# A decoder trunk's prologue on one core: high halves of the first units ahead of the modulated tiles, and conditioning tiles moved between the steps of layer 0

## The chip, the cores and the metric

The kernel runs on one core of one Trainium2 chip. The metric is the device time of one execution in microseconds (us). Times here come from repeated runs of the kernel and from one profiled execution. A core has TensorE (PE in the profile, its weight loads PEld), VectorE (DVE), ScalarE (ACT), GpSimd (POOL) and SyncE (SP), which here issues most transfers.

## The reference, cut to what matters

Two layers over 256 rows of width 2048, batch one. The conditioning vector c gives shift, scale and gate of both sub-layers through w_ada (2 x 2048 x 12288):

```
cond = silu(c)
for l in range(2):
    ada = cond @ w_ada[l] + b_ada[l]
    sh_m, sc_m, g_m, sh_f, sc_f, g_f = split(ada, 6)
    h = x * (1 + sc_m) + sh_m
    y = hybrid_mixer(h, ...)      # h @ w_in (6672 columns), three head groups, @ w_out
    x = layer_norm(alpha * x + (1 + g_m) * y)
    h = x * (1 + sc_f) + sh_f
    y = square(relu(h @ w1[l])) @ w2[l]
    x = layer_norm(alpha * x + (1 + g_f) * y)
```

The mixer's three groups are a retention, a gated linear recurrence (HGRN2, with masks at several levels) and a state space layer (Mamba-2) whose input goes through a causal convolution of four taps.

## The kernel before

**Units and passes.** Every weight matrix is read in units of 128 x 1024 f32 (0.5 MB). A layer has 25 passes of 16 units, 400 units; unit n belongs to pass n // 16. Passes 0 to 6 are the input projection (pass 3 has 528 columns only), 7 and 8 the output projection, the rest the MLP. A matmul in full precision is made of three: each weight W is split into a high half WH (ScalarE rounds it to fp32r, `hi_split`, line 735) and a low half WL = W - WH (VectorE subtracts, `lo_split`, line 1116), and each left operand likewise. Both splits run four units (`AHEAD`) in front of the matmuls. RAW and WL share nine slots, WH has six; SyncE loads unit n when unit n - 9 has been multiplied, and ScalarE's high half of unit n needs unit n - 6 multiplied.

**Conditioning tiles.** A tile is 128 of the columns of w_ada, turned, 128 x 2048 f32 (1 MB). VectorE makes its 128 values with one multiply-and-accumulate over 2048 elements, a dot. 32 tiles (shift and scale of the first sub-layer) are needed before the first matmul; they are the prologue. The other 160 are spread over the steps of VectorE's program: `tile_plan()` lists at which unit each dot stands, gives the tile one of seven slots (ONE, XA, XB, HA, HB, HC, KM) and the unit behind whose weights SyncE issues the tile's load, at least three units later in the order of the queue and at least eight behind the dot that last used the slot. HA to HC are free only when passes 0 to 6 are done, and x itself is loaded (by GpSimd, at unit 114) over the slots XA and XB when their last dot, at unit 112, is done.

**The prologue.** Eight batches b. In each, VectorE does four dots (`first_dot`, line 1347), makes the scale and shift columns of two tiles of h (`first_cols`, lines 1354 and 1355), then subtracts the low halves of the batch's first units (`FIRST_UNITS[b]`: two in batches 0 to 4, four in 5 to 7) and the low parts of the two tiles (`h_lo`, line 1122). Batches 1 and 2 hold small tables too. ScalarE does `first_tiles(b)`: two tiles of h, each written twice (lines 772 and 775), which wait for the columns; then the high halves of the batch's units. The matrix engine multiplies the batch's units (line 1643 for those of pass 0, 1675 for those of pass 1). SyncE issues the four tiles of a batch into four slots, each when the dot four before it is done, a 0.5 MB piece of the turned x in every second batch, and then the batch's units.

**The steps around the tiles.** Each engine's program goes through the units in order with the other work written in at fixed places. On VectorE a step does: a mask of the recurrence (`hg_mask`, lines 1333 to 1341; passes 2 and 3, units 7, 10, 13 and 15 of each), the low half of the unit four ahead, then the dots of that step (`dot`, line 1057), then the convolutions (pass 3, units 52, 53, 55, 56, 58, 59, 61, 62, and pass 4, units 67 to 70), and the rest of the head groups (line 1504: eight products of pass 5; lines 1536 and 1544: norm of the third group, pass 7). ScalarE and the matrix engine have their own lists, with semaphores between them. `GATE_DUE` says at which unit the matrix engine turns eight tiles' values into half a gate (`gate_sums`, line 1605); VectorE reads the sums two steps later (`gate_out`, line 1066), and the matrix engine waits for that three steps later. In layer 0 the second gate half of the mixer is due at unit 140, so the wait stands at 143, ahead of the last four units of pass 8, which are multiplied together by row and column quarter (`last_units`, line 1657).

Of the kernel before, what the change touches and what calls it, by code (L numbers as in the profile page):

```python
# [17 lines left out]
P = 128  # L18
# [6 lines left out]
UW = 1024  # L25
# [3 lines left out]
FIRST_UNITS = [[(0, 2 * b), (0, 2 * b + 1)] + ([(1, 2 * (b - EARLY_FROM)), (1, 2 * (b - EARLY_FROM) + 1)] if b >= EARLY_FROM else []) for b in range(8)]  # L29
# [15 lines left out]
LN_EPS, RMS_EPS = 1e-5, 1e-6  # L45


GATE_DUE = [{125: 4, 140: 5, 172: 10, 195: 11}, {106: 16, 134: 17, 172: 22, 195: 23}]
GATE_SEQ = [4, 5, 10, 11, 16, 17, 22, 23]
LATE = 14  # L50
ONE, XA, XB, HA, HB, HC, KM = range(7)
# [2 lines left out]
def tile_plan():  # L54

    both = [t for kt in range(KT) for t in (48 + kt, 64 + kt)]
    plan = [(0, [23, 25, 27, 29, 31, 33, 35, 37, 40, 42, 44, 46, 50, 55, 60, 66, 71, 76, 80, 83, 85, 88, 91, 94,
                 96, 98, 101, 103], both[:2 * LATE]),
            (0, [105, 107, 109, 112, 114, 117, 119, 121], range(32, 40)),
            (0, [124, 126, 128, 130, 132, 134, 136, 138], range(40, 48)),  # L60
            (0, [145, 148, 151, 154], both[2 * LATE:]),
            (0, [156 + 2 * k for k in range(8)], range(80, 88)),
            (0, [174 + 5 * k // 2 for k in range(8)], range(88, 96)),
            (0, [196 + 49 * k // 16 for k in range(64)],
             [96 + t for kt in range(KT) for t in (kt, 16 + kt)] + [96 + t for t in both]),
            (1, [80 + 3 * k for k in range(8)], [96 + t for t in range(32, 40)]),
            (1, [107 + 3 * k for k in range(8)], [96 + t for t in range(40, 48)]),
            (1, [145 + 3 * k for k in range(8)], [96 + t for t in range(80, 88)]),
            (1, [174 + 5 * k // 2 for k in range(8)], [96 + t for t in range(88, 96)])]
    tiles, last, uses = [], {}, {}  # L70
    for layer, steps, cols in plan:
        for n, t in zip(steps, cols):
            step, i = layer * NUNIT + n, 32 + len(tiles)
            if n >= FF0 * KT:
                slots = (ONE, KM)
            elif n >= 117:
                slots = (ONE, HA, HB, HC)
            else:
                slots = (ONE, XA, XB) if layer == 0 and n <= 112 else (ONE,)
            slot = min(slots, key=lambda k: last.get(k, (-1, 0))[0] if k in last else -1)  # L80
            prev = last.get(slot)
            load = max(step + 3, prev[0] + 8 if prev else 0, layer * NUNIT + 121 if HA <= slot <= HC else 0,
                       tiles[-1][4] if tiles else 0)
            assert load <= step + 11, (step, load)
            fresh = slot >= HA and (prev is None or prev[0] < layer * NUNIT + 112)
            uses[slot] = uses.get(slot, 0) + 1
            tiles.append((step, t, slot, uses[slot], load, prev[1] if prev else None, fresh))
            last[slot] = (step, i)
    return tiles
# [15 lines left out]
COL0 = [2048, 3072, 5120, 6144, 0, 1024, 4096]  # L105
# [43 lines left out]
def hybrid_trunk(nc, x, c, positions, lb_logits, w_in, w_out, w_ada, b_ada, ln_g, ln_b, hg_norm_w,  # L149
                 m_conv_w, m_conv_b, m_dt_bias, m_a_log, m_d, m_norm_w, w1, w2, consts, x_turned, out):  # L150
    with ExitStack() as ctx:
# [280 lines left out]
        w_in_r = w_in.rearrange("l k n -> (l k) n")  # L432
# [101 lines left out]
        @block.sync  # L534
        def _(sp):
            def tile_load(layer, i):
                _, t, slot, _, _, prev, fresh = TILES[i - 32]
                if prev is not None:
                    sp.wait_ge(dots.sem, prev + 1)
                if fresh:  # L540
                    sp.wait_ge(unit_done.sem, unit_done.at(layer, 7 * KT))
                sp.dma_start(tile_slot(i), w_ada_r[t]).then_inc(tile_in[slot].sem, 16)

            def raw_load(layer, n, src):
                slot = raw_slot(layer, n)
                if layer or n >= RAW_SLOTS:
                    sp.wait_ge(unit_done.sem, unit_done.at(layer, n + 1) - RAW_SLOTS)
                if len(src.shape) == 3:
                    dst = RAW[:, slot, :].rearrange("p (t n) -> p t n", t=2)
                else:  # L550
                    dst = RAW[:, slot, 0:src.shape[1]]
                sp.dma_start(dst, src).then_inc(raw_in[slot].sem, 16)

            sp.dma_start(CROW[:, :], c.squeeze(0).partition_broadcast(P)).then_inc(pro_crow.sem, 16)
            n = 0
            for b in range(8):
                for i in range(4 * b, 4 * b + 4):
                    if i >= PRO_SLOTS:
                        sp.wait_ge(dots.sem, i - PRO_SLOTS + 1)
                    sp.dma_start(FT[:, i % PRO_SLOTS, :], w_ada_r[i % 2 * 16 + i // 2]  # L560
                                 ).then_inc(pro_tile[i % PRO_SLOTS].sem, 16)
                    if i % 8 == 0:
                        t0 = i // 2
                        sp.dma_start(XT[:, t0:t0 + 4, 1, :], x_turned[t0 * P:(t0 + 4) * P, :].rearrange(
                            "(t p) n -> p t n", p=P)).then_inc(pro_xt.sem, 16)
                for p, kt in FIRST_UNITS[b]:
                    raw_load(0, n, w_in_r[kt * P:(kt + 1) * P, COL0[p]:COL0[p] + UW])
                    n += 1
            for layer in range(DEPTH):
                for p in range(FF0):  # L570
                    for kt in range(KT):
                        n = p * KT + kt
                        if layer == 0 and n < EARLY:
                            continue
                        if p < 7:
                            src = w_in_r[ds(layer * D + kt * P, P), COL0[p]:COL0[p] + width(p)]
                        else:
                            src = w_out_r[ds(layer * D + OUT_ORDER[kt] * P, P), (p - 7) * UW:(p - 6) * UW]
                        raw_load(layer, n, src)
                        for i in LOAD_AT.get(layer * NUNIT + n, ()):  # L580
                            tile_load(layer, i)
                for g in range(GROUPS):
                    for m in range(4 * KT):
                        s, kt = divmod(m, KT)
                        n = FF0 * KT + g * 64 + m
                        if split_unit(g, m):
                            src = w1_r[ds(layer * D + m % 8 * 2 * P, 2 * P), ds(g * D + m // 8 * 512, 512)
                                       ].rearrange("(t p) n -> p t n", p=P)
                        elif s < 2:
                            src = w1_r[ds(layer * D + kt * P, P), ds(g * D + s * UW, UW)]  # L590
                        else:
                            src = w2_r[ds(layer * DFF + g * D + kt * P, P), (s - 2) * UW:(s - 1) * UW]
                        raw_load(layer, n, src)
                        for i in LOAD_AT.get(layer * NUNIT + n, ()):
                            tile_load(layer, i)
            for i in range(8):
                r, ch = divmod(i, 4)
                sp.wait_ge(x_out.sem, i + 1)
                cols = slice(ch * 512, (ch + 1) * 512)
                sp.dma_start(out_r[:, r, cols], X[:, r, cols]).then_inc(out_done.sem, 16)  # L600
            sp.wait_ge(out_done.sem, 16 * 8)
# [97 lines left out]
        def _(act):  # L699
# [173 lines left out]
            act.activation(ACT_IDLE[:, :], PT[:, 0:1], ACT.Identity)  # L873
            n = 0
            for b in range(8):
                first_tiles(b)
                for _ in FIRST_UNITS[b]:
                    hi_split(0, n)
                    n += 1
                if b == 1:  # L880
                    act.wait_ge(pro_dve.sem, 1)
                    act.activation(LX[:, :], LX[:, :], ACT.Exp).then_inc(pro_act.sem, 1)
                    act.wait_ge(pro_dve.sem, 2)
                    act.activation(SIN[:, :, :], ANG[:, :, :], ACT.Sin).then_inc(pro_act.sem, 1)
                    act.activation(S2[:, :, :], ANG[:, :, :], ACT.Sin, scale=0.5).then_inc(pro_act.sem, 1)
            for n in range(EARLY, EARLY + AHEAD):
                hi_split(0, n)
            for layer in range(DEPTH):
                for p in range(FF0):
                    for kt in range(KT):  # L890
                        n = p * KT + kt
# [25 lines left out]
                        if p in (2, 3) and kt in HG_X1:  # L917
                            i = (p - 2) * 4 + HG_X1.index(kt)
# [9 lines left out]
                        if p in (2, 3) and kt in HG_M and HG_M.index(kt) % 2:  # L928
                            i = (p - 2) * 4 + HG_M.index(kt)
# [35 lines left out]
                        if p == 5 and kt in M_ARG:  # L965
                            i = M_ARG.index(kt)
# [42 lines left out]
                for g in range(GROUPS):  # L1009
# [15 lines left out]
                    for m in range(4 * KT):  # L1025
                        s, kt = divmod(m, KT)
                        n = FF0 * KT + g * 64 + m
# [989 lines left out]
```

## Time and profile before

| | us |
|---|---|
| median of 3 runs (lowest, highest) | 2494.16 (2489.54, 2495.68) |
| the profiled execution | 2494.9 |
| its span, first to last instruction | 2493.1 |
| PE busy | 2374.6 (95%) |
| DVE busy | 1898.1 (76%) |
| ACT busy | 1158.9 (46%) |
| POOL busy | 173.2 (7%) |

The span is what the trace covers; the time of the execution is 1.8 us more. A busy share is an average: the matrix engine is busy through nearly all stages and stands still in a few places, which the rows below show. Transfers moved 637.97 MB, 256 GB/s on average.

### The profile page before, as it was taken

The page shows a single profiled execution, that of the slowest core. Times are in us where ns is not written, and L with a number is a line of the kernel's source. Part 1 is how long each engine was busy: PE and PEld are TensorE (multiplying, and loading weights), DVE is VectorE, ACT ScalarE, POOL GpSimd, SP SyncE. Part 2 cuts the span into 40 slices and gives each one's busy share as a digit, 9 for nine tenths or more (in the row PEclk, how much of TensorE's full clock was granted, in tenths as well). Part 3 has the DMA queues.
Part 4 walks back from the last instruction along what each step waited for, and adds up shares of the span by engine and source line. Part 5 has one row for each costly group of instructions (what it writes and reads, how often), then busy time and mean ns, then how long its engine had stood idle before and what let it go on. Part 6 is the DMA issues. An engine that isn't in the chain of part 4 may idle for free.

```text
span 2493.1 us, 31995 instructions
## 1 busy us (share of the span) xinstructions
PE 2374.6 (95%) x12916; PEld 2055.3 (82%) x12916; DVE 1898.1 (76%) x2128; ACT 1158.9 (46%) x1505; POOL 173.2 (7%) x122
## 2 busy tenths in 40 slices
PE   2589999999999999999999999999999999999998
PEld 2579888778888888888879998888888888888886
DVE  5878987888998878888886578777888565655657
ACT  2254565635434434434446447554553443443442
POOL 0002100010011011020010110001001101101001
PEclk9799999999999999999999999999999999999999
DMA  8996677978999888888866446677788656656653
GB/s 343 368 344 232 208 262 265 336 301 283 341 354 319 304 322 310 311 318 312 310 195 184 146 121 210 228 272 258 267 283 288 190 189 194 186 190 192 186 192 118
DMA packets 179912, 637.97 MB, mean 256 GB/s; under 512 B 17260, under 2 KB 20020, under 8 KB 153780
## 3 DMA queue, kind: packets, MB, share of 16 engines
q1 hardware_dynamic: 174928, 617.94, 71.7%
q0 software_dynamic: 3296, 17.43, 1.9%
q8 instruction: 102, 1.67, 0.3%
q10 hardware_dynamic: 1540, 0.55, 0.1%
q14 instruction: 46, 0.38, 0.1%
HBM read 633.75 MB, written 2.10 MB: 255 GB/s over the span
## 4 chain that ended last, share of the span: by engine, by line
PE 86%; DVE 9%; ACT 2%; issue 1%; DMA 1%; ACTq 0%; DVEq 0%
PE PS L1675 44%; PE PS L1701 17%; PE PS L1703 9%; PE PS L1643 6%; PE PS L1684 4%; DVE WL L1116 3%; PE PS L1657 2%; DVE FT L1347 2%; DVE FH L1057 1%; DMA MD<-in_m_d 1%; ACT WH L735 1%; PE PS L1734 1%; DVE CV L1322 1%; PE PS L1626 0%; PE PS L1605 0%
## 5 line engine op out<-in xcount | busy, mean ns | idle before, releaser
L1116 DVE TENSOR_TENSOR WL<-RAW,WH 128x1024 fp32r<-128x1024 f32 (+1 forms) x800 | 995.7, 1256 | 494.3 <-ACT WH L735 492.5
L735 ACT ACTIVATE WH<-RAW 128x1024 fp32r<-128x1024 f32 (+1 forms) x800 | 829.9, 1043 | 1035.8 <-PE PS L1675 533.2
L1701 PE MATMUL PS<-HT,WH 128*128 128x512 f32 x1792 | 633.4, 399 | 0.0
L1703 PE MATMUL PS<-HT,WL 128*128 128x256 f32 x1792 | 503.1, 281 | 0.0
L1701 PEld LDWEIGHTS PS<-HT,WH 128*128 128x128 f32 x1792 | 336.7, 188 | 83.6
L1675 PE MATMUL PS<-WH,T2h 128*128 128x512 f32 x1208 | 373.3, 390 | 3.2 <-DVE T2l L1122 3.2
L1675 PE MATMUL PS<-WH,T2l 128*128 128x512 f32 x1208 | 372.7, 390 | 0.0
L1675 PE MATMUL PS<-WL,T2h 128*128 128x512 f32 x1208 | 372.6, 390 | 0.0
L1703 PEld LDWEIGHTS PS<-HT,WL 128*128 128x128 f32 x1792 | 338.5, 189 | 0.2
L1675 PE MATMUL PS<-WH,HT 128*128 128x512 f32 x1024 | 287.6, 394 | 0.6 <-issue 0.6
L1675 PEld LDWEIGHTS PS<-WH,T2h 128*128 128x128 f32 x1208 | 226.0, 188 | 50.5 <-DVE T2l L1122 4.1
L1675 PEld LDWEIGHTS PS<-WH,T2l 128*128 128x128 f32 x1208 | 227.2, 188 | 47.4
L1675 PEld LDWEIGHTS PS<-WL,T2h 128*128 128x128 f32 x1208 | 227.1, 188 | 47.4
L1675 PEld LDWEIGHTS PS<-WH,HT 128*128 128x128 f32 x1024 | 188.4, 188 | 38.8 <-issue 0.9
L1643 PE MATMUL PS<-HT,WH 128*128 128x256 f32 x1024 | 154.8, 303 | 66.0 <-DVE WL L1116 64.5
L623 POOL TENSOR_TENSOR X<-X,Y 128x512 f32<-128x512 f32 x64 | 113.9, 1811 | 1327.4 <-DVE Y L1280 1327.4
L1643 PEld LDWEIGHTS PS<-HT,WH 128*128 128x128 f32 x1024 | 142.2, 209 | 69.9 <-DVE WL L1116 66.7
L1057 DVE SCALAR_TENSOR_TENSOR FONE<-FONE,CROW 128x2048 f32<-128x2048 f32 x77 | 178.1, 2313 | 0.4 <-DMA FONE<-in_w_ada 0.3
L1675 PE MATMUL PS<-WL,HT 128*128 128x512 f32 x512 | 158.2, 390 | 0.0
L1684 PE MATMUL PS<-HT,WH 128*128 128x256 f32 x768 | 143.7, 287 | 0.0
L1684 PEld LDWEIGHTS PS<-HT,WH 128*128 128x128 f32 x768 | 120.0, 192 | 0.2
L1057 DVE SCALAR_TENSOR_TENSOR FK<-FK,CROW 128x2048 f32<-128x2048 f32 x50 | 115.3, 2306 | 0.1
(293 smaller groups left out, 2125.6 us busy)
## 6 DMA issues: line engine op xcount, KB each, us to landing
RAW<-in_w SPq DMA_DIRECT2D x512, 512.0 KB, 4.5
RAW<-in_w_in SPq DMA_DIRECT2D x192, 512.0 KB, 3.8
FONE<-in_w_ada SPq DMA_DIRECT2D x77, 1024.0 KB, 7.0
FK<-in_w_ada SPq DMA_DIRECT2D x50, 1024.0 KB, 6.9
FT<-in_w_ada SPq DMA_DIRECT2D x32, 1024.0 KB, 7.0
RAW<-in_w_out SPq DMA_DIRECT2D x64, 512.0 KB, 6.7
FX<-in_w_ada SPq DMA_DIRECT2D x21, 1024.0 KB, 6.1
FH<-in_w_ada SPq DMA_DIRECT2D x12, 1024.0 KB, 10.1
```

What stands on the lines that cost most here:

```text
L623: pool.tensor_tensor(xc, xc, Y4[:, b, :], ALU.add).then_inc(x_add.sem, 1)
L735: act.activation(WH[:, wh_slot(layer, n), 0:w], RAW[:, k, 0:w], ACT.Copy).then_inc(hi_done.sem, 1)
L1057: stt(w, w, 1.0, CROW[:, :], ALU.mult, ALU.mult, accum_out=ADA[:, ds(t, 1)]).then_inc(dots.sem, 1)
L1116: tt(WL[:, k, 0:w], RAW[:, k, 0:w], WH[:, wh_slot(layer, n), 0:w].bitcast(F32), ALU.subtract).then_inc(lo_done.sem, 1)
L1322: ins = stt(dst[:, j, sh:SEQ], src[:, j, 0:SEQ - sh], cCW[:, tap, t:t + 1], dst[:, j, sh:SEQ], ALU.mult, ALU.add)
L1347: stt(w, w, 1.0, CROW[:, :], ALU.mult, ALU.mult, accum_out=ADA[:, ds(i % 2 * 16 + i // 2, 1)]).then_inc(dots.sem, 1)
L1643: ins = mm(dst, w[:, slot[w is WL], j * P:(j + 1) * P], a[:, kt, :], start=first and i == 0 and j % 2 == 0, stop=last and i == 2, skip_gro ...
L1657: ins = mm(bank(p, q)[:, :], a[:, kt, rows], w[:, slot[w is WL], h * 512:(h + 1) * 512], start=False, stop=n == units[-1] and i == 2)
L1675: ins = mm(bank(p, 2 * r + h)[:, :], a[:, kt, rows], w[:, slot[w is WL], h * 512:(h + 1) * 512], start=first and i == 0, stop=last and i == 2)
L1684: ins = mm(dst, w[:, slot[w is WL], cols], a[:, kt, :], start=first and i == 0 and j % 2 == 0, stop=last and i == 2, skip_group_check=True)
L1701: mm(bank(p, j)[:, :], WH[:, wh, cols], HT[:, kt, :, :], start=kt == 0, stop=False, skip_group_check=True)
L1703: ins = mm(bank(p, j)[:, SEQ:2 * SEQ], WL[:, wl, cols], HTh[:, kt, :], start=False, stop=kt == KT - 1, skip_group_check=True)
```

## The change

Four edits. ScalarE makes the high halves of a batch's units before the batch's modulated tiles, not after them. SyncE issues a batch's units between its second and third tile (i % 4 == 1) and not behind its fourth. In layer 0, the 44 dots up to unit 138 are spread anew: fifteen stand up to unit 49 where thirteen stood up to 50, none between 50 and 65 (before: 50, 55, 60), and those of 66 to 138 now stand at 66 to 130, closer together, with the loads and slots that the planner derives from them. The second gate half of the mixer in layer 0 is due at unit 134 and not 140. Layer 1 keeps its steps.

```diff
-GATE_DUE = [{125: 4, 140: 5, 172: 10, 195: 11}, {106: 16, 134: 17, 172: 22, 195: 23}]
+GATE_DUE = [{125: 4, 134: 5, 172: 10, 195: 11}, {106: 16, 134: 17, 172: 22, 195: 23}]
...
-    plan = [(0, [23, 25, 27, 29, 31, 33, 35, 37, 40, 42, 44, 46, 50, 55, 60, 66, 71, 76, 80, 83, 85, 88, 91, 94,
-                 96, 98, 101, 103], both[:2 * LATE]),
-            (0, [105, 107, 109, 112, 114, 117, 119, 121], range(32, 40)),
-            (0, [124, 126, 128, 130, 132, 134, 136, 138], range(40, 48)),
+    plan = [(0, [23, 25, 27, 29, 31, 32, 33, 35, 36, 39, 42, 45, 47, 48, 49, 66, 70, 77, 79, 81, 83, 85, 87, 89,
+                 92, 94, 96, 98], both[:2 * LATE]),
+            (0, [100, 101, 103, 106, 107, 109, 111, 112], range(32, 40)),
+            (0, [117, 118, 120, 121, 123, 124, 126, 130], range(40, 48)),
...
-                for p, kt in FIRST_UNITS[b]:
-                    raw_load(0, n, w_in_r[kt * P:(kt + 1) * P, COL0[p]:COL0[p] + UW])
-                    n += 1
+                    if i % 4 == 1:
+                        for p, kt in FIRST_UNITS[b]:
+                            raw_load(0, n, w_in_r[kt * P:(kt + 1) * P, COL0[p]:COL0[p] + UW])
+                            n += 1
...
             for b in range(8):
-                first_tiles(b)
                 for _ in FIRST_UNITS[b]:
                     hi_split(0, n)
                     n += 1
+                first_tiles(b)
```

## Rows read from the trace of the kernel before

**Rows 1.** Waits of PE, whole run: us in total, times, longest us.
```profile
PE PS L1643 <- DVE WL L1116: 64.5, 8, 15.9
...
PE PS L1657 <- issue: 3.4, 1, 3.4
```

**Rows 2.** Timeline of the prologue: start us, us, engine, line, operation, [idle before].
```profile
26.70 0.20 ACT L728 ACTIVATE AL<-AL 16x2 f32<-16x2 f32 x1 [9.48 <-DMA MD<-in_m_d]
...
29.93 2.36 DVE L1116 TENSOR_TENSOR WL<-RAW,WH 128x1024 fp32r<-128x1024 f32 x2 [7.56 <-ACT WH L735]
...
32.88 2.29 DVE L1347 SCALAR_TENSOR_TENSOR FT<-FT,CROW 128x2048 f32<-128x2048 f32 x1
...
41.92 0.15 DVE L1355 SCALAR_TENSOR_TENSOR SC<-ADA,PT 128x2 f32<-128x2 f32 x1
...
44.09 1.99 ACT L735 ACTIVATE WH<-RAW 128x1024 fp32r<-128x1024 f32 x2
45.16 2.36 DVE L1116 TENSOR_TENSOR WL<-RAW,WH 128x1024 fp32r<-128x1024 f32 x2 [3.09 <-ACT WH L735]
...
137.79 2.29 DVE L1347 SCALAR_TENSOR_TENSOR FT<-FT,CROW 128x2048 f32<-128x2048 f32 x1
...
140.00 2.29 DVE L1347 SCALAR_TENSOR_TENSOR FT<-FT,CROW 128x2048 f32<-128x2048 f32 x1
...
145.65 4.63 DVE L1116 TENSOR_TENSOR WL<-RAW,WH 128x1024 fp32r<-128x1024 f32 x4 [3.09 <-ACT WH L735]
```

**Rows 3.** Windows: busy us of PE, PEld, DVE, ACT, POOL, granted clock, DMA share, GB/s.
```profile
12.00:34.00 22.00, 3.78 (x17) 3.50 (x18) 11.42 (x15) 5.98 (x10) 0.00 (x0) 1.00 1.01 405
60.00:125.00 65.00, 36.78 (x216) 34.92 (x216) 52.45 (x75) 17.67 (x26) 0.00 (x0) 0.73 0.95 368
90.00:120.00 30.00, 16.49 (x98) 16.00 (x99) 23.76 (x27) 9.83 (x14) 0.00 (x0) 0.72 1.01 397
343.30:365.70 22.40, 22.40 (x101) 17.47 (x100) 22.40 (x22) 14.49 (x22) 0.00 (x0) 1.00 0.86 318
486.90:491.90 5.00, 4.95 (x15) 3.92 (x16) 3.34 (x9) 4.63 (x10) 0.85 (x2) 0.66 0.93 382
549.00:556.00 7.00, 5.54 (x13) 4.41 (x14) 1.25 (x3) 0.00 (x0) 0.00 (x0) 0.52 0.21 88
```

**Rows 4.** Timeline of pass 3 in layer 0, VectorE and the matrix engine.
```profile
257.22 0.93 DVE L1116 TENSOR_TENSOR WL<-RAW,WH 128x528 fp32r<-128x528 f32 x1 [2.27 <-ACT WH L735]
...
278.71 0.49 PE L1748 MATMUL PS<-V,SM 128*128 128x128 f32 x2 [2.83 <-DVE SM L1341]
...
284.95 2.29 DVE L1057 SCALAR_TENSOR_TENSOR FX<-FX,CROW 128x2048 f32<-128x2048 f32 x1
...
290.60 0.49 PE L1748 MATMUL PS<-V,SM 128*128 128x128 f32 x2 [2.46 <-DVE SM L1341]
```

**Rows 5.** Timeline of pass 5: the first product and the matmul that takes it.
```profile
364.86 0.95 DVE L1504 TENSOR_TENSOR MW<-MW,SB 128x768 f32<-128x768 f32 x1
...
366.07 0.43 PE L1878 MATMUL PS<-XD,MW 128*128 128x64 f32 x2
```

**Rows 6.** Timeline of pass 7: the dot of unit 114 and the waits behind it.
```profile
466.39 2.28 DVE L1057 SCALAR_TENSOR_TENSOR FONE<-FONE,CROW 128x2048 f32<-128x2048 f32 x1
...
477.75 1.94 PE L1758 MATMUL PS<-K,XS 128*128 128x128 f32 x16 [1.69 <-DVE XS L1544]
...
480.82 1.06 ACT L735 ACTIVATE WH<-RAW 128x1024 fp32r<-128x1024 f32 x1 [2.71 <-DMA RAW<-in_w_out]
...
486.95 0.73 PE L1675 MATMUL PS<-WH,T2h 128*128 128x512 f32 x2 [1.79 <-DVE T2l L1122]
```

**Rows 7.** Timeline of pass 8: VectorE reads the gate's sums.
```profile
548.97 1.28 DVE L1066 SCALAR_TENSOR_TENSOR GB<-PS,GB 128x512 f32<-128x512 f32 x2
```

**Rows 8.** The chain that ended last: start us, us, what, at two sub-layers' last four units.
```profile
550.46 13.84 PE PS L1657 x48
...
1278.27 10.89 PE PS L1657 x48
```

## Prediction

> **What bounds the kernel now.** I read the waits of the matrix engine first: where it stands still, and for whom, since it is busy for nearly the whole span. The reader is to see one large sum, 64.5 us in eight waits for the low halves of the first weights, and one wait of 3.4 us that the profile puts to nobody [rows 1]; smaller ones stand in passes 3 and 7 of layer 0 [rows 4, 6]. Everything between the eight batches of the prologue and those places is continuous matmul work, so only what moves these waits moves the end. Then I read the timeline at each. In a prologue batch VectorE does four dots of 2.21 us from start to start, the columns, and then stands 3.09 us until ScalarE has made two modulated tiles twice over and the first high half, and only then subtracts; the engine that sets the pace idles for the helper [rows 2]. The windows say what the transfers have left: 397 to 405 GB/s where they are dense, 368 over the batches from 60 to 125 us [rows 3].
>
> **The prologue, ScalarE's order.** With the high halves first, they are ready long before the columns, except in batch 0. What VectorE then does per batch is four dots 8.85, columns 0.25, two subtractions and two tile differences 3.0 (from 29.93 to the next dot at 32.88): 12.1 us where it now takes 15.2. The 3.09 goes from batches 1 to 7. In batch 0 ScalarE is free only at 26.9 us, after the last small table [rows 2]; two high halves (2.0), then four tile operations (2.0) end at 30.9, so the last difference ends at 31.2 and the dots of batch 1 begin there in place of 32.9: 1.6 us. If VectorE alone set the pace, its last dot would end 1.6 + 6 x 3.09 = 20.1 us earlier, at 122.2 in place of 142.3, and the matrix engine would start batch 7 another 3.09 earlier: 23.2 us.
>
> **The prologue, transfers.** A tile of w_ada is 128x2048 f32, 1.05 MB, a first unit 128x1024, 0.52 MB, a quarter of the turned x 0.52 MB. From the ninth tile on there are 24 x 1.05 + 18 x 0.52 + 3 x 0.52 = 36.2 MB until the last tile lands, since the units of a batch now stand ahead of its third and fourth tile in SyncE's queue. The ninth tile can be asked for when the fifth dot is done, 1.6 us earlier than at 35.1 us, so the stream starts at about 35.2. From then on four tile slots are asked for again as the dots go, and in the 3.3 us that VectorE spends on differences up to 4 MB are outstanding: the stream doesn't stop. At 400 GB/s (between the two dense windows of [rows 3]) it takes 90.5 us, the last tile lands at 125.7, its dot ends at 128.0: 14.3 us earlier than now. That is later than VectorE's 122.2, so from about batch 5, where four units are loaded and not two, the tiles set the pace. With the 3.09 of the last batch the matrix engine is 17.4 us earlier in batch 7 and from there on. Bounds: 23.2 (VectorE's pace) and, at 385 GB/s, 94.0 us of stream, 13.9.
>
> The Trainium skill ("DMA: Bandwidth & Descriptors", Specifications) gives about 358 GB/s as a core's HBM limit, which speaks against this change: by it the stream would take 101 us and the gain be 6.8 us. The trace does not agree: its dense windows are above it by a tenth [rows 3].
>
> ScalarE's new order can block: the high half of a batch's last unit needs the slot of the unit six before. In batch 7 that is a unit of batch 6, whose matmuls start some 15 us before batch 7's columns; costed at nothing, and if that unit is late, batch 7 waits the difference. The moved load issues (22 of 0.4 us) stand where SyncE waits for dots anyway.
>
> **Dots out of the convolutions.** Now dots stand at units 50, 55 and 60; the last two lie right before masks for which the matrix engine then waits 2.83 and 2.46 us [rows 4]. With both gone VectorE's chain is 2 x 2.21 = 4.4 us shorter. Against it, three dots now stand at 47, 48, 49 and none at 46 or 50: VectorE would come to the subtraction at 257.2 with 2.9 us more work behind it, but it stands idle 2.27 there, waiting for ScalarE [rows 4]; so it is 0.6 late. That leaves 3.8; bounds 2.2 (one dot's worth) and 5.3, both waits gone.
>
> **Denser dots after them.** Units 66 to 98 now hold one more dot until unit 85: 66, 70, 77, 79, 81, 83, 85 in place of 66, 71, 76, 80, 83, 85. That extra 2.2 us comes ahead of the first product of pass 5, which now ends 0.3 us before the matrix engine takes it [rows 5], and VectorE is busy through the 22 us before [rows 3]. So the matrix engine will wait 1.9 us where it waits nothing now: a loss of 1.9, up to 3.6 if its clock falls as behind the wait in pass 7 [rows 3]. The later products have a wider margin, or a dot less in front of them.
>
> **Pass 7.** The dot of unit 114 stands right before the product that the norm of the third head group needs [rows 6]; moved to 111, it gives the chain 2.2 us, and the wait of 1.69 for the transposed rows goes. But the next one, for the low tiles, is held by ScalarE too, which stands 2.71 us for weights in a dense stretch of transfers, and now two tiles of w_ada are ahead of one of them. I let the low tiles come 2.1 us earlier in all; bounds 0 and 3.9 (both waits and the slow matmuls after them: 5 us at 0.66 granted behind the second wait, so 1.7 lost [rows 3]).
>
> **Pass 8.** Dots at 128, 132, 134, 136, 138 are gone, 11 us of VectorE's work, and the gate's half is summed at unit 134 and read at 136. Now VectorE comes to it only at 549, after all the subtractions [rows 7], and the matrix engine, which may not start its last four units before, waits 3.44. Its granted clock is 0.52 in the stretch behind, near the lower of its levels, 1.2 GHz [rows 3], and the last 48 matmuls take 13.84 us where the same 48 take 10.89 in the next layer boundary [rows 8]. Both go: 3.4 + 2.95 = 6.4, bounds 3.4 and 6.4. The 16 matmuls of the gate's sum are as many as before.
>
> **Costed at nothing.** Other moved dots and their loads: each tile's load is still at least three units behind its dot's, and the weights behind it in the queue have nine slots, 9 x 2.7 us of matmul work (48 matmuls are four units [rows 8]). Were that cover gone, each tile would cost its 1.05 MB at 400 GB/s, 2.6 us. The three moved into passes 2 and 3 fall into idle time of VectorE. Layer 1 has the same steps.
>
> **Sum.** 17.4 + 3.8 - 1.9 + 2.1 + 6.4 = 27.8 us. The profiled execution took 2494.9 (span 2493.1), so 2467.1; the median of the runs is 0.7 lower, which gives 2466.
>
> **Rivals.** (1) VectorE keeps the pace: transfers do better than 400 GB/s. 5.8 us more, 2460; with waits and clock in passes 5 and 7 at their better bounds 2455. For it: the two limits are only 5.8 us apart. Chance 0.2. (2) The stream is slower, since tiles now queue behind units and each dot waits for its own: at the 368 GB/s of the batches now, 98.4 us of stream, 7.9 more, 2474; with the poorer bounds of passes 3, 5 and 7, 2480. For it: the transfer engines are at 0.95 there already [rows 3]. Chance 0.2. The skill's 358 GB/s of the page above would give 2477 in place of 2474. (3) Slower than before, by handshakes. In passes 2, 3 and 5 the matrix engine takes a VectorE result at each of 16 steps; a dot that falls ahead of one costs 2.2 us, and 1.7 more if the clock falls. I find one such; from eight on the whole gain is gone, and eleven give 2507. Against it: in pass 5 the matrix engine waits for none of them now, and most are well ahead. Chance 0.03. (4) The change doesn't do what it says: ScalarE is held by slots or landed weights, so the 3.09 stays. Then 2494 - 10.4 = 2484; chance 0.05. Forecast, 2461 to 2472: 0.52.
>
> **Numbers.** 0.3% is 7.5 us, what a measurement of this kernel can tell from no change. Faster by more: the forecast, (1), (2) and all but a part of (4), 0.95; same 0.02; slower 0.03, from (3). The range reaches to the bounds of (1) and (2): 2455 to 2479.
>
> **What would show it.** In the profile after: VectorE's subtractions in the prologue with no idle time to ScalarE ahead of them from batch 1 on, and some to the tiles' transfers in batches 5 to 7; the eight waits near 47 in place of 64.5; the last dot of the prologue near 128; the masks' waits in pass 3 under 3 us in sum; a new wait of about 2 us for the first product of pass 5; no wait ahead of the last four units of pass 8, and 48 of them in 10.9 us. If the last dot of the prologue ends after 135, the transfers are the reason I am wrong; if pass 5 shows several waits, the denser dots are.

## The result, and the profile after

The changed kernel takes 2480.3 us (median of 5 runs, 2479.1 to 2481.8), 13.9 us less than before; the ratio to before is 0.9949, 95% interval 0.9933 to 0.9964. The forecast was 28 us, 2466 with a range from 2455 to 2479: the direction was right, half of the gain is missing, and the time lies 1.3 us outside the range. The profiled execution spans 2480.0 us, 13.1 less than before. Lines of the changed kernel stand one further than before (1643 is 1644, and so on).

I read the waits of the matrix engine first, then the chain of work that ended last, and took from it the time at which the same matmuls start in both kernels. That gives the gain by stage.

The waits of PE over the whole run (engine, line, what it waited for: us in total, times, longest):

```profile
PE PS L1644 <- DVE WL L1117: 35.5, 7, 7.5
PE PS L1644 <- ACT HT L773: 14.6, 1, 14.6
...
PE PS L1676 <- issue: 7.5, 2, 7.2
PE PS L1749 <- DVE SM L1342: 6.3, 4, 2.1
PE PS L1879 <- DVE MW L1505: 3.5, 3, 1.9
PE PS L1676 <- DVE T2l L1123: 2.9, 2, 1.5
PE PS L1644 <- DVE HT L1123: 2.4, 2, 1.6
```

Against [rows 1]: the waits of the prologue, ten now, are 35.5 + 14.6 + 2.4 = 52.5 us in place of 64.5, and the wait of line 1657 is gone. In its place stands a new one of 7.2 us at line 1676 that the profile puts to nobody ("issue"), and a wait for products of pass 5.

The prologue in the chain of the changed kernel (start us, us, what):

```profile
69.18 11.47 DMA FT<-in_w_ada
...
114.61 12.76 DMA FT<-in_w_ada
...
127.38 2.31 DVE FT L1348 x2
...
129.95 4.54 DVE WL L1117 x4
...
134.88 5.90 PE PS L1644 x32
140.78 19.07 PE PS L1676 x84
```

The chain goes through the tiles' transfers, four times; the last dot ends at 129.7 (before 142.3, [rows 2]). The long run of pass 1 begins at 140.78; in the kernel before it began at 154.78, so 14.0 us are gained here. The same prologue began pass 1 between 138.6 and 140.8 in the traces of runs 1, 5, 6, 7 and 9, so this figure is good to about 2 us.

The timeline of PE at five places, in the order of time, shows where gain goes and comes:

```profile
255.25 0.79 PE L1749 MATMUL PS<-V,SM 128*128 128x128 f32 x2 [2.10 <-DVE SM L1342]
...
352.19 0.43 PE L1879 MATMUL PS<-XD,MW 128*128 128x64 f32 x2 [1.94 <-DVE MW L1505]
...
385.55 0.43 PE L1879 MATMUL PS<-XD,MW 128*128 128x64 f32 x2 [0.76 <-DVE MW L1505]
...
473.27 0.73 PE L1676 MATMUL PS<-WH,T2h 128*128 128x512 f32 x2 [1.47 <-DVE T2l L1123]
...
504.32 1.19 PE L1676 MATMUL PS<-WH,T2h 128*128 128x512 f32 x2 [7.17 <-issue]
```

In pass 3 the wait for a mask stands at 255 and no longer at 279 and 291 [rows 4]; the last mask is taken at 274.71, 15.9 us earlier than in [rows 4]. At the first product of pass 5 (352.19 for 366.07, [rows 5]) 13.9 are left, at line 1898 in pass 6 11.5 (412.11 for 423.58), at the low tiles of pass 7 13.7 (473.27 for 486.95, [rows 6]), and at the gate's sums behind unit 125, where the slow matmuls of [rows 3] lie behind the kernel before, 15.3 (489.73 for 505.01). Then comes the wait of 7.2 us, and the four rows behind it, at 0.50 of the clock, take 1.5 us more than at full clock. Pass 8 ends without a wait, in the chain:

```profile
540.63 10.89 PE PS L1658 x48
```

It ends 12.8 us earlier than in [rows 8], which is what is left of the gain.

What the matrix engine waits for at 504 is read in the same chain, upstream of it:

```profile
476.32 16.34 DMA RAW<-in_w_out
...
493.65 2.85 ACT X L903 x2
...
497.26 1.05 ACT WH L736
...
498.34 0.98 DVE WL L1117
...
499.48 2.29 DVE FH L1058 x2
501.77 1.15 DVE WL L1117
...
504.32 2.04 PE PS L1676 x4
```

The weights of unit 129 take 16.3 us from their issue to landing. Those of unit 128 are late too: ScalarE stands 7.44 us for them, then scales x (3.7 us) ahead of the next high half, and a dot of 2.3 us stands between two subtractions on VectorE. The piece of 1.40 us that the chain calls "issue" has a name in VectorE's timeline (first line ScalarE's, then VectorE's):

```profile
491.48 2.27 ACT L736 ACTIVATE WH<-RAW 128x1024 fp32r<-128x1024 f32 x2 [7.44 <-DMA RAW<-in_w_out]
...
492.57 1.23 DVE L1117 TENSOR_TENSOR WL<-RAW,WH 128x1024 fp32r<-128x1024 f32 x1 [3.71 <-ACT WH L736]
...
502.82 1.28 DVE L1067 SCALAR_TENSOR_TENSOR GB<-PS,GB 128x512 f32<-128x512 f32 x2
```

The last line is VectorE reading the sums of the first gate half, due at unit 125. It does so in step 127, behind the low half of unit 131, and the matrix engine may not start unit 128 before the read is done. The read ends at 504.10, the matmul starts at 504.32. Unit 128's own low half (the line at 492.57) had been there since 493.80, and the matrix engine had come to it at 497.15. So the wait is one for the gate's read, held up by late weights, and not one for the weights of the unit that is multiplied. The other traces bear this out: the read ends and unit 128 starts at 517.58 and 517.82 in run 4, 496.98 and 497.20 in run 5, 497.98 and 498.19 in run 7. In the kernel before the read ended at 511.24 and unit 128 began at 512.27, so there was 1.0 us to spare. The wait ahead of the last four units of pass 8, which the profile also puts to nobody, is of the same kind ([rows 7, 8]: the read ends at 550.25, the matmuls start at 550.46).

The window over this stretch says what the transfers do, 414 GB/s over 50 us at a busy share of 1.01, while the matrix engine works 41 of 50 us (columns as in [rows 3]):

```profile
455.00:505.00 50.00, 41.36 (x197) 34.16 (x196) 40.44 (x50) 27.58 (x42) 1.71 (x4) 0.96 1.01 414
```

### The profile page after: what moved, and what is told of

Same layout as the page of the kernel before. It is cut to its first block, busy times and chain, and to the rows that moved or that the text cites. A ratio compares the mean times of both kernels' runs of the same rounds, so it can differ in the third digit from the quotient of the medians.

```text
span 2480.0 us, 31995 instructions
## 1 busy us (share of the span) xinstructions
PE 2371.3 (96%) x12916; PEld 2052.9 (83%) x12916; DVE 1898.5 (77%) x2128; ACT 1161.7 (47%) x1505; POOL 167.3 (7%) x122
## 4 chain that ended last, share of the span: by engine, by line
PE 84%; DVE 9%; DMA 3%; ACT 1%; issue 1%; ACTq 0%; DVEq 0%
PE PS L1676 42%; PE PS L1702 17%; PE PS L1704 9%; PE PS L1644 6%; PE PS L1685 4%; DVE WL L1117 2%; DMA FT<-in_w_ada 2%; PE PS L1658 2%; DVE FT L1348 1%; DMA MD<-in_m_d 1%; DVE FX L1058 1%; PE PS L1735 1%; DMA RAW<-in_w_out 1%; DVE CV L1323 1%; DVE FONE L1058 1%
## 5 line engine op out<-in xcount | busy, mean ns | idle before, releaser
L1644 PE MATMUL PS<-HT,WH 128*128 128x256 f32 x1024 | 152.6, 300 | 53.9 <-DVE WL L1117 35.5
```

What stands on the lines that cost most here:

```text
L1644: ins = mm(dst, w[:, slot[w is WL], j * P:(j + 1) * P], a[:, kt, :], start=first and i == 0 and j % 2 == 0, stop=last and i == 2, skip_gro ...
```

## The experiments

Each ratio is to the kernel before, measured beside it on the same chip. An interval is about 0.0013 wide to either side, 3 us.

**1 to 4. The prologue alone, its two halves, and the rest alone.** The edits are the hunks of the diff ahead of the prediction:

```diff
e1: kernel before + hunk of SyncE's loads + hunk of ScalarE's order
e2: kernel before + hunk of ScalarE's order
e3: kernel before + hunk of SyncE's loads
e4: changed kernel - these two hunks (GATE_DUE and tile_plan() alone)
```

> The kernel before with both prologue edits (ScalarE's high halves first, SyncE's first units ahead of the third and fourth tile) and nothing else. Theory: the prologue is worth 14.0 us, as the start of the pass behind it shows in the changed kernel (140.78 in place of 154.78), and the rest of the change is worth nothing in sum: 2494.2 - 14.0 = 2480.2, from 2478 to 2482. Rival: the rest of the change is worth several us by itself, since waits moved by the earlier prologue (dots against products) took part of it: then this one is slower than the changed kernel, 2484 or more. Second rival: the rest of the change costs, because the weights of pass 7 come late only with the new list of steps: 2478 or less.

Measured: 2479.6 us, ratio 0.9936 (0.9924 to 0.9949). As the theory said.

> The kernel before with only ScalarE's order changed (high halves ahead of the modulated tiles); the loads stay behind the batch's four tiles. Theory: the units then land some 12 us behind the previous batch's last dot, about when the columns are there, so the high halves start late and hold the tiles back; a part of the gain stays, about 7 us: 2487, 2483 to 2491; the 3.09 us of idle time ahead of VectorE's subtractions shrinks but does not go. Rival: ScalarE's order is all of it, the moved loads are worth nothing: 2480, idle gone.

Measured: 2475.8 us, ratio 0.9923 (0.9909 to 0.9936). Theory and rival were both wrong: ScalarE's order alone gives 19.5 us, more than with the loads moved. In its timeline VectorE, after batch 0, waits for tiles in one batch only, three times, and for ScalarE 0.41 us in each of the last four batches:

```profile
99.79 0.42 DVE L1122 TENSOR_TENSOR HT<-TX,HT 128x256 fp32r<-128x256 f32 x1 [0.41 <-ACT TX L775]
103.22 2.29 DVE L1347 SCALAR_TENSOR_TENSOR FT<-FT,CROW 128x2048 f32<-128x2048 f32 x1 [0.79 <-DMA FT<-in_w_ada]
105.70 2.29 DVE L1347 SCALAR_TENSOR_TENSOR FT<-FT,CROW 128x2048 f32<-128x2048 f32 x1 [0.18 <-DMA FT<-in_w_ada]
108.19 2.29 DVE L1347 SCALAR_TENSOR_TENSOR FT<-FT,CROW 128x2048 f32<-128x2048 f32 x1 [0.19 <-DMA FT<-in_w_ada]
...
123.33 2.28 DVE L1347 SCALAR_TENSOR_TENSOR FT<-FT,CROW 128x2048 f32<-128x2048 f32 x1
```

Its last dot ends at 125.6 where that of e1 ends at 130.9. The four units of the last batch are 2.1 MB, 5.2 us at 405 GB/s, and in e2 they stand behind the last tile and not ahead of it. The matrix engine starts pass 1 at 137.5 (e1: 140.3); half of the difference is given back since the units are late for ScalarE. In the traces of runs 2, 10, 11 and 12, which all have this prologue, pass 1 starts between 134.7 and 137.5, and with the loads moved never before 138.6.

> The kernel before with only the first units' loads moved ahead of a batch's third and fourth tile. Theory: ScalarE still makes tiles first, so the 3.09 us per batch stays, and the tiles have slack at that pace: 2494, within 2 us, or 1 to 2 us slower by batch 0, where the last two dots are 2.2 us later. Rival: the units' early landing alone lets ScalarE split earlier: 2490 or less.

Measured: 2495.0 us, ratio 1.0000 (0.9991 to 1.0009): nothing, as the theory said. The 3.09 us stand in every batch behind the first. So the moved loads give nothing without ScalarE's order, and cost about 3 to 4 us with it (3.8 by the medians of e1 and e2, 3.2 by the ratios).

> The changed kernel with the prologue of before: the new list of steps and the gate's due unit alone. Theory: gains of 1.9 in pass 3, 2.2 at the transposed rows and 6.3 in pass 8, against 4.4 in pass 5 and 7 to 8 in pass 7: 2494.2 + 1 = 2495, from 2492 to 2498, with a wait of about 7 us for weights ahead of the last matmuls of pass 7. Rival: the 7 us wait in pass 7 is made by the earlier prologue and not by the list of steps: then 2487.

Measured: 2497.9 us, ratio 1.0011 (1.0002 to 1.0021), 2.5 us slower than its before; the wait, which stands at the border of passes 7 and 8, is there:

```profile
PE PS L1675 <- issue: 5.5, 1, 5.5
PE PS L1675 <- DVE T2l L1122: 2.7, 1, 2.7
```

The theory holds: the new steps of the dots are worth nothing in sum, whether the prologue is early or not, and the wait at unit 128 comes from them.

**5. The layer norm's loads moved behind the wait.**

```diff
-                        if at == (7, 12):
-                            pool.wait_ge(t2_ready.sem, t2_ready.at(layer, 16))
-                            pool.wait_ge(x_res.sem, x_res.at(layer, 0))
-                            load_ln(layer, 0)
                         if at == (8, 2):
                             add_y(layer, 0, 0)
+                            pool.wait_ge(t2_ready.sem, t2_ready.at(layer, 16))
+                            pool.wait_ge(x_res.sem, x_res.at(layer, 0))
+                            load_ln(layer, 0)
```

> The changed kernel with GpSimd's loads of the layer norm's scale and offset (2 x 1.05 MB, at 477.4 in it) moved from the thirteenth unit of pass 7 to behind the third unit of pass 8, when the matrix engine has passed the 7.2 us wait; 505 to 510 moves only 16 GB/s. Theory: the 7.2 us wait at 497 to 504 is one for weights whose transfers stand in line with 21 MB in 50 us at 417 GB/s; 2.1 MB less ahead of them is 5.0 us, so the wait falls to about 2 and the time to 2475 (2473 to 2477). Rival: SyncE issues these weights late (481 to 489) because it stands behind tile loads that wait for dots, and the transfers are not the limit: then the time stays at 2480, and 2 MB less change the wait by under 1 us.

Measured: 2488.9 us, ratio 0.9974 (0.9963 to 0.9986), 8.6 us slower than the changed kernel by the medians, and not the 5 us faster that I expected. But the wait at 497 to 504 is gone as the theory said: the matrix engine goes on at 497.20 after 0.5 us. What makes it slower is another wait of 5.3 us, in pass 8 at unit 137, for the read of the second gate half, which the chain (first) and ScalarE's timeline (second) show:

```profile
522.60 1.23 ACT LNB L802
...
524.40 1.05 ACT WH L735
...
527.83 1.21 DVE GB L1066 x2
529.08 10.64 PE PS L1675 x36
```

```profile
520.78 1.92 ACT L801 ACTIVATE LNG<-LNG 128x2048 f32<-128x2048 f32 x1 [8.54 <-DMA LNB<-in_ln_b]
```

ScalarE prepares the layer norm's scale and offset in pass 8, ahead of the high halves of its last units. I had read when the layer norm needs them (551) and not who touches them before. It stood 8.54 us for them, and all that is queued behind it stood too. It is the same in layer 1 (a second wait, of 6.2 us). For the question asked the answer is clear: with 2.1 MB less to move, 6.7 of the 7.2 us go, so the bytes make the weights late. The two loads need not stand ahead of the weights for that. In the changed kernel GpSimd issues them in its own queue at 477.4, after SyncE has asked for unit 129 at 476.32, and unit 129 still takes 16.3 us; without them it is asked for at 475.87 and ScalarE has it at 485.33. The rival is a small part at most: in the changed kernel SyncE asks for unit 130 at 481.43, 2.4 us after its slot came free, because it stands behind a tile's load that waits for a dot; for unit 131 it is 0.2 us late.

**6. The dots of pass 5 as before.**

```diff
-                47, 48, 49, 66, 70, 77, 79, 81, 83, 85, 87, 89, 92, 94, 96, 98], both[:2 * LATE]),
-            (0, [100, 101, 103, 106, 107, 109, 111, 112], range(32, 40)),
+                47, 48, 49, 66, 71, 76, 80, 83, 85, 88, 90, 92, 94, 95, 97, 98], both[:2 * LATE]),
+            (0, [100, 102, 104, 106, 107, 109, 111, 112], range(32, 40)),
```

> The changed kernel with the dots between units 66 and 90 at the steps of before (71, 76, 80, 83, 85, 88 in place of 70, 77, 79, 81, 83, 85, 87, 89), and the one dot that this leaves over caught up at 90 to 99. Theory: the waits for two products of pass 5 (1.9 and 0.8) and the slow matmuls behind them go, 4.4 us in all: 2476 (2474.5 to 2478), unless the later wait in pass 7 takes back a part, since it is a wait for transfers that keep their own time. Rival: that is just what happens: what the matrix engine gains in pass 5 it waits more in pass 7, and the time stays within 1 us of 2480.

Measured: 2483.8 us, ratio 0.9952 (0.9940 to 0.9965): not better, by the medians 3.5 worse. The first product is no longer waited for (349.53 in place of 352.19, 2.7 us earlier). But one dot of my own list, at unit 90, stands ahead of a product and a sum that were free of dots before:

```profile
374.22 0.66 PE L1879 MATMUL PS<-XD,MW 128*128 128x64 f32 x2 [1.89 <-DVE XS L1513]
...
397.50 0.70 PE L1676 MATMUL PS<-WH,HT 128*128 128x512 f32 x2 [0.86 <-issue]
```

In the ten us from 370 the granted clock is 0.70, and the gain is gone by 397. The wait of 7.0 us at unit 128 is unchanged, so the rival is not what happened either. The run does not price pass 5; it shows what one dot in the wrong place costs there. Run 12 has the list without it.

**7. The last eight tiles spread.**

```diff
-            (0, [117, 118, 120, 121, 123, 124, 126, 130], range(40, 48)),
+            (0, [117, 119, 121, 124, 126, 128, 130, 132], range(40, 48)),
```

> The changed kernel with the last eight dots of the gate's half at 117, 119, 121, 124, 126, 128, 130, 132 in place of 117, 118, 120, 121, 123, 124, 126, 130; the gate stays due at 134. Theory: three of the eight tiles (1.05 MB each) are asked for two to five units later, so the weights of the end of pass 7 have 2 to 3 MB less ahead of them; the 7.2 us wait falls by 4 to 7, 2475 (2472 to 2477). Rival: the gate's half then comes late in pass 8 and a wait of about 2 to 3 us ahead of its last four units comes back: 2478 to 2481.

Measured: 2474.9 us, ratio 0.9918 (0.9904 to 0.9931), 5.4 us better than the changed kernel. As the theory said; the wait at unit 128 is

```profile
498.19 0.84 PE L1676 MATMUL PS<-WH,T2h 128*128 128x512 f32 x2 [2.12 <-issue]
```

and the second gate half, due at 134, is still in time. The median time of a unit's weights from issue to landing, from 440 to 500 us, is 13.2 us in the changed kernel, 10.4 here, 9.2 in run 5, and 8.4 in the kernel before (455 to 515).

**8. Half the bytes of the prologue's tiles.**

```diff
+                    wd = D if i < 8 else D // 2
-                    sp.dma_start(FT[:, i % PRO_SLOTS, :], w_ada_r[i % 2 * 16 + i // 2]
+                    sp.dma_start(FT[:, i % PRO_SLOTS, 0:wd], w_ada_r[i % 2 * 16 + i // 2][:, 0:wd]
```

> The changed kernel, but from the ninth tile of the prologue on only the first half of each tile is loaded (0.52 MB in place of 1.05; the modulation's columns are computed from what the slot holds, so the output is not the reference's). Theory: the transfers set the pace of the last batches; with 12.6 MB less, VectorE's waits for tiles (7 us from the third batch on) go, its last dot ends near 122.7 in place of 129.7, and the matrix engine starts the pass behind the prologue 7 us earlier, 2473 or a little more where later waits keep their own time. Rival: the tiles are late because SyncE issues them late, one by one behind the dots, and not for their bytes: then at least half of the waits stay.

Measured: 2473.4 us, ratio 0.9910 (0.9897 to 0.9924). From the third batch on one wait for a tile is left, 0.42 us; the last dot ends at 121.4, and pass 1 begins at 130.74, 10.0 us earlier than in the changed kernel. 7 of them are left at the end; where the other 3 go no run shows. The transfers' bytes set the pace in the changed kernel, and not SyncE's issuing tiles one by one behind the dots, and VectorE's own pace is the 122 of the forecast.

**9. The gate's due unit alone.**

```diff
-GATE_DUE = [{125: 4, 134: 5, 172: 10, 195: 11}, ...
+GATE_DUE = [{125: 4, 140: 5, 172: 10, 195: 11}, ...
```

> The changed kernel with only the last gate half's due unit put back from 134 to 140; the dots stand as in it, so all eight are done by unit 130. Theory: the early due unit is worth what the trace of before shows at the end of pass 8, a wait of 3.4 us and 48 matmuls in 13.84 us in place of 10.89; both come back: 2480.3 + 6.4 = 2486.7, from 2485 to 2488. Rival: VectorE's 11 us of dots at 128 to 138 made the sums late and not the due unit, so with the dots gone the wait stays away or is half as long: 2483 or less.

Measured: 2486.5 us, ratio 0.9966 (0.9953 to 0.9978). By the medians 6.2 us, the theory's; by the ratios 4.2; and in the trace less. The timeline of PE has

```profile
542.44 0.47 PE L1658 MATMUL PS<-WH,T2h 128*128 128x512 f32 x1 [2.04 <-issue]
```

and in the chain

```profile
542.44 12.76 PE PS L1658 x48
```

A wait of 2.0 and 1.9 us of slow matmuls, 3.9 in all, where the kernel before has 6.4. The due unit is worth about 4 us by the trace and the ratios (whose intervals are 3 us wide to either side), and the absence of the dots the rest; the runs do not part the two more finely.

**10 to 12. Better versions.** e10 keeps the kernel before but for ScalarE's order and a gate at 137; e11 adds the dots moved out of the convolutions; e12 is the changed kernel with its costly parts mended.

```diff
e10: ScalarE's order;  140: 5 -> 137: 5
-            (0, [124, 126, 128, 130, 132, 134, 136, 138], range(40, 48)),
+            (0, [123, 124, 126, 128, 130, 132, 134, 135], range(40, 48)),
e11: e10 and
-[23, 25, 27, 29, 31, 33, 35, 37, 40, 42, 44, 46, 50, 55, 60, 66,
+[23, 25, 27, 29, 31, 32, 33, 35, 36, 39, 42, 45, 47, 48, 49, 66,
e12: changed kernel - hunk of SyncE's loads, and
+ ... 47, 48, 49, 66, 71, 76, 80, 83, 85, 88, 91, 93, 95, 97, 98, 100], both[:2 * LATE]),
+            (0, [102, 103, 105, 107, 108, 110, 111, 112], range(32, 40)),
+            (0, [117, 119, 121, 124, 126, 128, 130, 132], range(40, 48)),
```

> The kernel before with three things: ScalarE's order (as measured alone: 2475.8), the last gate half due at 137 in place of 140, and its last eight dots at 123, 124, 126, 128, 130, 132, 134, 135 in place of 124 to 138; all other dots and both load orders stay. Theory: the gate's gain does not need the dense list: the sums at 137 leave the matrix engine three units, 8 us, of other work before the wait, so 6.4 us come on top and pass 7 gets at most one tile more: 2469.4, from 2468 to 2472. Rival: the tiles asked for one to three units earlier delay the weights of passes 7 and 8 as in the changed kernel: 2474 or more.

Measured: 2472.3 us, ratio 0.9914 (0.9900 to 0.9927). 3.5 us better than ScalarE's order alone, not 6.4. The wait ahead of pass 8's last units is gone, and in the profiled execution, the longest of its five, waits of 3.4 us ("issue") and of 4.0 us for a mask stand where ScalarE's order alone has 0.3 and 2.8. The 3.4 us stand at unit 128, where the gate's read ends at 498.50 and the matmul starts at 498.72. So tiles asked for one to three units earlier are felt there, which is the rival in part. The mask's 4.0 us lie in pass 3, ahead of every step that this run changes; they belong to this one execution, which is 5.5 us above the median.

> The kernel of the run before this one, with the dots of 50, 55 and 60 moved as in the changed kernel (fifteen up to unit 49), those from 66 on as before. Theory: pass 3 alone gives what the changed kernel's trace shows, 1.9 us, since three dots in a row at 47, 48, 49 make a mask late at 255 where later ones were late before: 1.9 under the run before this one. Rival: without the denser dots behind it the full 3.8 us of the forecast come; or none, if the gain is waited for at a later transfer.

Measured: 2468.9 us, ratio 0.9899 (0.9886 to 0.9913), 3.4 us better than e10 by the medians. The traces show less: from the start of pass 1 to the first product of pass 5 it takes 209.5 us here (137.49 to 346.95) and 211.4 with ScalarE's order alone (137.54 to 348.90), which is 1.9, as in the changed kernel. The trace of e10 cannot serve for this, because of its mask. So the theory's 1.9 stands, and the medians, each good to 3 us, do not speak against it.

> The changed kernel with each costly part mended: the first units' loads behind the batch's tiles again (measured: 3.8 us better with ScalarE's order alone), the last eight dots at 117, 119, 121, 124, 126, 128, 130, 132 (measured: 5.4 better), and the dots from 66 on at 66, 71, 76, 80, 83, 85, 88, 91, 93, 95, 97, 98, 100 and 102, 103, 105, 107, 108, 110, 111, 112, so that none stands ahead of a product of pass 5 that stood behind it before. Theory: 2480.3 - 3.8 - 5.4 - 4.4 (pass 5) = 2466.7, from 2465 to 2470. Rival: the dots left over stand so close from 97 to 112 that the transfers, at 415 GB/s from 400 to 450 us already, are late for passes 6 and 7 instead: 2471 or more, with a new wait there.

Measured: 2466.4 us, ratio 0.9888 (0.9875 to 0.9902), as the theory said: 28.4 us better than its before by the medians, twice the gain of the change as made. Its profiled execution starts pass 1 at 134.7, 2.9 us before that of run 2 with the same prologue, so a part of the close match may be luck. The waits from 130 to 700 us:

```profile
PE PS L1748 <- DVE SM L1341: 3.5, 2, 2.1
PE PS L1675 <- DVE T2l L1122: 1.8, 1, 1.8
PE PS L1878 <- DVE MW L1504: 0.7, 1, 0.7
...
PE PS L1675 <- issue: 0.3, 1, 0.3
```

No long wait of the matrix engine is left in pass 7 or at unit 128, and the 50 us from 450 move 401 GB/s.

## Why the prediction was half right

| step of the prediction | forecast | in the traces |
|---|---|---|
| prologue, to the start of pass 1 | 17.4 | 14.0 |
| dots out of the convolutions | 3.8 | 1.9 |
| denser dots, pass 5 | -1.9 | -4.4 |
| pass 7, low tiles and clock | 2.1 | 3.8 |
| "Costed at nothing": loads and weights | 0 | -8.9 |
| pass 8 | 6.4 | 6.4 |
| sum | 27.8 | 12.8 |

The last column is worked out from equal matmuls in both traces. The 3.8: from 11.5 in pass 6 to 15.3 us of gain at the gate's sums of unit 125. The -8.9: from these 15.3 to the last units of pass 8, which start at 540.63, 6.4 before the 547.0 (550.46 less its wait of 3.4) at which the kernel before came there. The last row but one: 3.4 of wait and 13.84 - 10.89. Spans differ by 13.1, medians by 13.9. (One sum of the forecast is short of a term: rival 1 reaches 2455 only with the better bound of pass 3 as well, 2460 - 1.9 - 1.8 - 1.5.)

**The step that failed** is "Costed at nothing". It said that the weights behind a tile in the queue have nine slots, 9 x 2.7 us, as cover, and so put other loads and dots at nothing; they cost 8.9 us. For the matmuls of the late units the cover held: the low halves of units 128 to 131 were done at 493.8, 497.2, 499.6 and 502.9. From 497.15 on, at 2.72 us a unit, the matrix engine would have asked for them at 497.2, 499.9, 502.6 and 505.3. That is an estimate from the traces' times; no run moves the first gate half's due unit to test it. What had less cover is the read of the first gate half. The step never named it. VectorE reads behind the low half of unit 131, and unit 128 waits for the read. SyncE may ask for unit 131 when unit 122 is done, so from there to unit 128 are five units, 13.6 us, and the high half, the low half and the read take 3.6 of them. The median unit took 8.4 us from issue to landing in the kernel before, which left 1.0 us at the read, and 13.2 in the changed one, 16.3 for the unit in the chain. The wait is 7.2 us, and slow matmuls behind it make most of the rest.

Run 7 shows the cause by spreading the tiles (5.4 back), run 5 by taking other bytes out of the stretch (6.7 of the 7.2 us wait gone), run 4 that the new steps bring it by themselves. I had looked at the transfers where they were dense and not added up a stretch: from 450 to 490 us the changed kernel issues fourteen units of weights (7.3 MB), eight tiles (8.4), x (2.1), half a gate's bias (0.5) and the layer norm's two rows (2.1): 20.4 MB, and 414 GB/s move 16.6 in 40 us.

**ScalarE's order** was right: the 3.09 us are gone in batches 1 to 7, and run 8 shows VectorE's own pace at 121.4 where the forecast had 122.2.

**The transfers** were right as the bound, from batch 4 on, and forecast a little too fast: the last tile landed at 127.36 and not at 125.7. The 36.2 MB took 92 us from 35.2, 393 GB/s where I took 400. What the prediction did not ask is whether the loads had to be moved: it took their bytes ahead of the tiles as given, and counted only SyncE's time for their issue as the cost. Run 2 shows the kernel without them, 3 to 4 us faster. By the Trainium skill ("DMA: Bandwidth & Descriptors", Specifications), with its 358 GB/s for a core, the gain was to be 6.8 us; the trace does not agree, 414 GB/s over 50 us. Another page of the Trainium skill ("Perfetto Trace Analysis", Roofline) says that this share holds when both cores of a pair are active and that one core alone can reach about 120% of it; the trace agrees, at 116%.

**The last batch.** The matrix engine starts it 15.8 us earlier (131.14 for 146.93), and 1.8 us are lost inside it. The windows of the changed kernel show the granted clock at half, which is the lower of its two levels, 1.2 GHz, for 5 us. They begin 1.4 us behind a stop of 1.80 us of an engine that had been at full clock, and a second stop of 0.79 us falls into them:

```profile
132.50:135.00 2.50, 1.71 (x9) 1.42 (x8) 2.50 (x4) 1.47 (x2) 0.00 (x0) 0.50 1.00 419
135.00:137.50 2.50, 2.50 (x12) 2.50 (x13) 2.43 (x3) 0.44 (x1) 0.00 (x0) 0.50 1.09 425
137.50:140.00 2.50, 2.50 (x17) 2.50 (x17) 1.23 (x1) 0.62 (x1) 0.00 (x0) 0.70 0.97 380
```

In the kernel before only one window of 2.5 us is that low (0.51, from 147.5) behind its stop of 4.19. I had counted no clock here.

**Dots out of the convolutions.** Size off. The three dots in a row at 47, 48, 49 hold VectorE from 233.5 to 241.4, and the mask behind them is late at 255.25. The 2.27 us of idle time that I set against them was not all there; how much of it was, no run shows.

**Pass 5.** The wait of 1.9 us came where and as long as forecast. The clock falls behind it (0.79 granted from 350 to 358), which I had kept for the bound of 3.6, and a second product, at unit 92, has a dot right ahead of it that it did not have before: 0.8 more. "A wider margin, or a dot less in front of them" was not looked up product by product.

**Pass 7's low tiles and pass 8.** The low tiles come 2.2 us earlier, as forecast, and the slow matmuls behind them, which I had kept for the bound of 3.9, are gone too: 3.8. Pass 8's 6.4 came as forecast, though run 9 puts a part of it down to the dots' absence.

**Luck.** The step at nothing lost more than the whole list of steps could win: 1.9 - 4.4 + 3.8 - 8.9 + 6.4 = -1.2 us. That the change is faster at all, and comes within 1.3 us of the range, is the prologue's doing.

## What to carry to other kernels

Before moving loads closer together, add up the bytes of the whole stretch and set them against the time that the prefetch really has: from the issue to whatever the busiest engine waits for behind it, which can be another engine's work that stands later in the same program, as the gate's read does here, and not the matmul on the loaded data. A wait that the profile puts to nobody can be found by looking for what ended just before it. A load that is moved ahead of another one costs its bytes there, even when its issue is free (run 2 against run 1); moving it pays only if somebody waits for it. And moving a helper's work off a chain (ScalarE's order, one hunk) was worth more than the whole change.

## What the hardware showed unasked

While GpSimd adds to x, VectorE's instructions are longer: in run 5 the dot of 503.57 takes 3.38 us, where it takes 2.29 elsewhere, beside GpSimd's four additions from 500.01 to 508.1.

```profile
503.57 3.38 DVE L1057 SCALAR_TENSOR_TENSOR FONE<-FONE,CROW 128x2048 f32<-128x2048 f32 x1
...
500.01 8.09 POOL L624 TENSOR_TENSOR X<-X,Y 128x512 f32<-128x512 f32 x4 [34.36 <-DVE Y L1280]
```

The granted clock fell to its lower level behind stops of about 2 us as well as behind longer ones: in the changed kernel it is 0.50 behind the stops of 1.80 (at 131.14) and 2.10 us (at 255.25). It is 1.00 in the 2.5 us behind those of 1.50 (at 274.71) and 1.47 (at 473.27). A longer stop need not cost more: the clock is low for 5 us behind the stop of 1.80, and for 2.5 us behind the 4.19 of the kernel before.
